# Memory values of a two-block transformer kernel: projection blocks 512 columns wide, into two PSUM banks

## The reference, cut

```python
def memory_cross_attention(x, mem_n, w_q, w_k, w_v, w_o):
    q = (x @ w_q).reshape(B, S, XA_HEADS, XA_DH)
    k = (mem_n @ w_k).reshape(B, -1, XA_HEADS, XA_DH)
    v = (mem_n @ w_v).reshape(B, -1, XA_HEADS, XA_DH)
    s = jnp.einsum('bshd,bmhd->bhsm', q, k).astype(jnp.float32) * (XA_DH ** -0.5)
    p = jax.nn.softmax(s, axis=-1).astype(x.dtype)
    o = jnp.einsum('bhsm,bmhd->bshd', p, v).reshape(B, S, D_MODEL)
    return o @ w_o
```

## Time and profile before

| | us |
|---|---|
| median of the runs (lowest, highest) | 1287.16 (1286.42, 1287.82) |
| profiled execution, its own time | 1286.86 |
| its span | 1284.8 |
| PE busy | 1267.4 (99%) |
| DVE busy | 829.8 (65%) |
| ACT busy | 661.7 (52%) |
| bytes read from HBM | 215.71 MB, 169 GB/s |

### The profile page before, as it was taken

How to read it: one execution, slowest core, us unless ns; L and a number is a source line. 1 busy time by engine, 2 the same in 40 slices (tenths; PEclk the granted TensorE clock), 3 DMA queues, 4 the chain that set the end, 5 groups by cost and what they waited for, 6 DMA issues and landing times.

```text
span 1284.8 us, 17262 instructions
## 1 busy us (share of the span) xinstructions
PE 1267.4 (99%) x6852; PEld 1093.4 (85%) x6852; DVE 829.8 (65%) x1269; ACT 661.7 (52%) x999; POOL 27.6 (2%) x32
## 2 busy tenths in 40 slices
PE   9999999999999999999999999999999999999997
PEld 8888888898788888899989997888888998888886
DVE  5655666878667565668988665755556564755554
ACT  6454546667574444453526644644445654644443
POOL 0000000010000000000000000000001000000000
PEclk9999999999999999999999999999999999999999
DMA  8655555452355555544424542655554442655551
GB/s 298 204 184 181 191 186 194 162 170 82 113 178 190 184 192 184 184 161 164 148 83 150 187 134 97 250 184 191 186 190 155 165 148 82 213 196 184 192 184 62
DMA packets 61854, 217.87 MB, mean 170 GB/s; under 512 B 6608, under 2 KB 9936, under 8 KB 61264
## 3 DMA queue, kind: packets, MB, share of 16 engines
q1 hardware_dynamic: 61488, 216.29, 50.2%
q10 hardware_dynamic: 288, 0.49, 0.1%
HBM read 215.71 MB, written 1.05 MB: 169 GB/s over the span
## 4 chain that ended last, share of the span: by engine, by line
PE 91%; DVE 6%; ACT 1%; DMA 1%; issue 0%; SPq 0%; POOL 0%; DVEq 0%; ACTq 0%
PE bank L1915 27%; PE bank L1917 26%; PE bank L1916 26%; DVE arena L1737 3%; DVE w_lo L1115 2%; PE bank L2117 1%; PE bank L1937 1%; PE bank L2254 1%; PE bank L2214 1%; PE bank L2003 1%; DMA w_raw<-weights_d 1%; PE bank L2225 1%; PE bank L2037 0%; PE bank L2246 0%; PE bank L2208 0%
## 5 line engine op out<-in xcount | busy, mean ns | idle before, releaser
L1115 DVE TENSOR_TENSOR w_lo<-w_raw,w_hi 128x1024 fp32r<-128x1024 f32 x383 | 467.6, 1226 | 343.7 <-ACT w_hi L583 342.3
L583 ACT ACTIVATE w_hi<-w_raw 128x1024 fp32r<-128x1024 f32 x383 | 404.1, 1059 | 475.6 <-PE bank L1917 454.8
L1915 PE MATMUL bank<-w_hi,x_hi 128*128 128x512 f32 (+2 forms) x928 | 361.3, 389 | 3.0 <-DVE w_lo L1115 2.4
L1917 PE MATMUL bank<-w_hi,x_lo 128*128 128x512 f32 (+2 forms) x928 | 356.6, 384 | 0.0
L1916 PE MATMUL bank<-w_lo,x_hi 128*128 128x512 f32 (+2 forms) x928 | 356.1, 384 | 0.0
L1915 PEld LDWEIGHTS bank<-w_hi,x_hi 128*128 128x128 f32 x928 | 175.1, 189 | 37.4 <-DVE w_lo L1115 3.6
L1917 PEld LDWEIGHTS bank<-w_hi,x_lo 128*128 128x128 f32 x928 | 175.1, 189 | 34.4
L1916 PEld LDWEIGHTS bank<-w_lo,x_hi 128*128 128x128 f32 x928 | 175.3, 189 | 32.6
L1915 PE MATMUL bank<-w_hi,h_hi 128*128 128x512 f32 (+1 forms) x364 | 142.4, 391 | 0.0
L1917 PE MATMUL bank<-w_hi,h_lo 128*128 128x512 f32 (+1 forms) x364 | 141.3, 388 | 0.0
L1916 PE MATMUL bank<-w_lo,h_hi 128*128 128x512 f32 (+1 forms) x364 | 141.3, 388 | 0.0
(11 more groups left out here) (312 smaller groups left out, 1440.0 us busy)
## 6 DMA issues: line engine op xcount, KB each, us to landing
w_raw<-weights_d SPq DMA_DIRECT2D x395, 512.0 KB, 3.3
arena<-weights_d SPq DMA_DIRECT2D x4, 512.0 KB, 6.2
arena<-ln_rows_d SPq DMA_DIRECT2D x2, 1024.0 KB, 5.5
arena<-late_d SPq DMA_DIRECT2D x1, 1056.0 KB, 5.7
xs<-x_d SPq DMA_DIRECT2D x2, 512.0 KB, 5.6
kv_mem<-mem_d SPq DMA_DIRECT2D x1, 1024.0 KB, 8.0
out_d<-xs SPq DMA_DIRECT2D x4, 256.0 KB, 2.4
cst<-cst_d SPq DMA_DIRECT2D x1, 671.0 KB, 7.2
```

The costliest lines, as they stand in the source:

```text
L583: nc.scalar.activation(w_hi[:, slot(b), :], w_raw[:, b % RAW, :], ACT.Copy).then_inc(hi_ready, 1)
L1115: nc.vector.tensor_tensor(w_lo[:, slot(b), :], w_raw[:, b % RAW, :], w_hi[:, slot(b), :].bitcast(F32), ALU.subtract).then_inc(lo_ready, 1)
L1915: nc.tensor.matmul(out, wh, xh, start=start, stop=False, skip_group_check=True)
L1917: return nc.tensor.matmul(out, wl, xh, start=False, stop=stop, skip_group_check=True)
```

## The change

The values are computed in blocks of 512 columns. A block now holds 2 x 128 rows of the inner length by 512 columns of weights, four blocks in a row (g = 0: m = 8 to 11, g = 1: m = 12 to 15) accumulate 512 of the 1024 value columns, for the two halves of the tokens in two banks, by 12 matmuls 512 columns wide per block instead of 24 of 256. ACT copies both banks after the fourth block (two copies of 128x512). The banks are 6 and 7, but 2 and 3 for g = 0 of layer 1. PE waits before the first block of a group: in layer 0 for mem_evac of 8 (all keys) and of 10 (both copies of g = 0), in layer 1 for g = 1 for both normalisations of layer norm 8. The query projection of layer 1 starts in bank 2 instead of 6, and waits at its start for 22 copies (before 23) and at c = 4 for 24 (before at c = 2). The row sums of the diff heads go to the second half of bank 5, ahead of weighted(5), and DVE reads them before head_lo(5). The host lays the weights of the values out to fit.

```diff
-        XQ_BANK = ((1, 3, 6, 7, 4, 5, 6, 7), (6, 3, 4, 5, 6, 7, 6, 7))
+        XQ_BANK = ((1, 3, 6, 7, 4, 5, 6, 7), (2, 3, 4, 5, 6, 7, 6, 7))
...
-        def fill_bank(l, m, k):
-
-            return PB[(2 if l == 1 and 8 <= m < 14 else 4 if l == 1 and m < 2 else 6) + k % 2]
+        def k_bank(l, m):
+
+            return PB[(4 if l == 1 and m < 2 else 6) + m % 2]
+
+        def v_bank(l, g):
+
+            return PB[2:4] if l == 1 and g == 0 else PB[6:8]
+
+        do_sums = PB[5][:, S:2 * S]
...
                     if m < DC:
                         done(b)
-                        nc.scalar.activation(k_mem[l][:, m, :], fill_bank(l, m, m)[:, 0:S], ACT.Copy).then_inc(mem_evac, 1)
-                    elif m % 2:
-                        c = (m - DC) // 2
+                        nc.scalar.activation(k_mem[l][:, m, :], k_bank(l, m)[:, 0:S], ACT.Copy).then_inc(mem_evac, 1)
+                    elif m % 4 == 3:
+                        g = (m - DC) // 4
                         done(b)
-                        nc.scalar.activation(v_mem[l][:, :, c * S:(c + 1) * S],
-                                             fill_bank(l, m, c)[:, :].rearrange("p (t n) -> p t n", n=S),
-                                             ACT.Copy).then_inc(mem_evac, 1)
+                        for t in range(2):
+                            nc.scalar.activation(v_mem[l][:, t, g * HALF:(g + 1) * HALF], v_bank(l, g)[t][:, :], ACT.Copy
+                                                 ).then_inc(mem_evac, 1)
...
+                if i == 8:
+                    dve.wait_ge(do_stat, 1)
+                    dve.wait_ge(o_ps, 6)
+                    dve.wait_ge(mla_hi, 2)
+                    link(nc.vector.tensor_scalar(rv[0:32, 0:S], do_sums[0:32, :], 1.0 / DIFF_V, RMS_EPS, ALU.mult, ALU.add))
+                    rsqrt_guess(rows[:, 0:S], rv[0:32, 0:S])
                 if i >= 3:
                     head_lo(i - 3, HEADS[i - 3])
-                if i == 8:
-                    dve.wait_ge(do_stat, 1)
-                    link(nc.vector.tensor_scalar(rv[0:32, 0:S], PB[6][0:32, 0:S], 1.0 / DIFF_V, RMS_EPS, ALU.mult, ALU.add))
-                    rsqrt_guess(rows[:, 0:S], rv[0:32, 0:S])
...
                     b = blk()
-                    o = m if m < DC else DC + (m - DC) // 2
-                    if o >= 2:
-                        pe.wait_ge(mem_evac, 12 * l + o - 1)
                     if m < DC:
-                        chunk(b, fill_bank(l, m, m)[:, 0:S], m_hi, m_lo)
-                    else:
-                        values(b, fill_bank(l, m, o), m % 2, m_hi, m_lo)
+                        if m >= 2:
+                            pe.wait_ge(mem_evac, 12 * l + m - 1)
+                        chunk(b, k_bank(l, m)[:, 0:S], m_hi, m_lo)
+                        continue
+                    g, i = (m - DC) // 4, m % 4
+                    if i == 0:
+                        pe.wait_ge(mem_evac, 12 * l + DC + (2 if l == 0 and g else 0))
+                        if l and g:
+                            pe.wait_ge(na_ready, 2 * LN[8] + 2)
+                            pe.wait_ge(nd_ready, 2 * LN[8] + 2)
+                    arrived(b)
+                    for k in range(2):
+                        for t in range(2):
+                            c, q, w = 2 * i + k, slice(t * P, (t + 1) * P), slice(k * HALF, (k + 1) * HALF)
+                            ins = three(v_bank(l, g)[t][:, :], m_hi[:, c, q], m_lo[:, c, q], w_hi[:, slot(b), w], w_lo[:, slot(b), w],
+                                        start=i == 0 and k == 0, stop=i == 3 and k == 1)
+                    ins.then_inc(block_done, 1)
...
-                pe.wait_ge(mem_evac, 19 if l == 0 else 23)
+                pe.wait_ge(mem_evac, 19 if l == 0 else 22)
                 for c in range(DC):
                     b = blk()
-                    if c == 3 - l:
+                    if c == 3 + l:
                         pe.wait_ge(mem_evac, 20 if l == 0 else 24)
...
+                if i == 7:
+                    for h in range(DIFF_HEADS):
+                        pe.wait_ge(do_sq, h + 1)
+                        ins = row_sums(do_sums[0:32, :], "rows_all", h, xs[:, h, 1, :], h == 0, h == DIFF_HEADS - 1)
+                    ins.then_inc(do_stat, 1)
                 if i >= 2:
                     weighted(i - 2, HEADS[i - 2])
-                if i == 7:
-                    pe.wait_ge(mem_evac, 11)
-                    for h in range(DIFF_HEADS):
-                        pe.wait_ge(do_sq, h + 1)
-                        ins = row_sums(PB[6][0:32, 0:S], "rows_all", h, xs[:, h, 1, :], h == 0, h == DIFF_HEADS - 1)
-                    ins.then_inc(do_stat, 1)
...
-    mem = [np.concatenate([columns(x["xa_wk_2"][l]), row_values(x["xa_wv_2"][l])]) for l in range(2)]
+    mem = [np.concatenate([columns(x["xa_wk_2"][l]), token_blocks(x["xa_wv_2"][l], HALF, 2).reshape(DC, P, BLK)]) for l in range(2)]
```

## The result

| | before | after |
|---|---|---|
| median of the runs beside each other, us | 1287.35 | 1291.68 |
| ratio (95% interval) | | 1.0035 (1.0024 to 1.0046) |
| span of the profiled execution, us | 1284.8 | 1289.9 |
| matmuls recorded on PE | 6852 | 6660 |

The account below looks back on a forecast made before the run. TensorE bounds the kernel, busy 1267.4 of 1284.8 us. Wait +5.15, blocks 12 to 15 -0.5, scores(8) -0.4, layer 1 -1.0, clock +1.5: +4.7 on 1287.16, so 1291.9 us, range 1289.4 to 1294.0.

Parts of the forecast that it names:

- The clock: Behind block 12's pause in layer 0, the granted clock falls to 0.50 for a while: 1.5 us lost.
- The wait at block 12: In layer 0, PE waits for both first-half copies, queued behind exponentials(3): idle about 5.7 us, block 12 starts 5.15 later.
- Nothing takes it up: During block 12's wait nothing else can run: PE is in order and later work queues behind it; delay 4.8 to 5.5 us.
- My bounds, 0.4 and 3: Clock loss after block 12's pause: near 0.4 us if slow time falls partly into it, near 3 if a second follows.
- The nines of the earlier trace: Profile page of the kernel before, read as TensorE at the full granted clock in all 40 slices.
- The wide matmuls: Value blocks of both layers: 0.13 us gained a block, 16 blocks, 2.1 us in all, ends 1.9 and 2.4.
- rival (c): Wide matmuls in the value blocks gain only about 0.03 us a block: +6.3, 1293.5 us; chance 0.05.
- slow first matmul of a group: Value blocks: a group's first matmul is slow, and a block standing alone pays it in either form; gain taken 0.13, not 0.15.
- L784's wait: Layer 0, scores(8): PE's 0.32 us idle on ACT's exponentials goes, as ACT no longer evacuates after block 13: -0.4 us.
- next late there is PE itself: At scores(8) of layer 0, once the wait on ACT's exponentials goes, PE is the next late: -0.4 us.
- Row sums and layer 1: Sums ahead of layer 0's weighted(5): cost 0, up to 0.5 without cover; layer 1's value blocks gain 1.0 us, layer-norm wait met.
- Rival (d): ACT evacuates block 11 ahead of exponentials(3): pause 1.4 us, sum -1.1, 1286.1; sign changes below a 2.5 us pause; chance 0.04.

Follow-up runs that it names:

- first and third experiments: First: kernel after, block 11's copies right behind exponentials(2), 1284.91 us. Third: kernel before, block 12 of layer 0 waiting for mem_evac 10 instead of 9, 1294.75 us.
- busy pause: Kernel after, with 42 unused 256-column matmuls on PE ahead of the wait at block 12 of layer 0: 1289.88 us, ratio 1.0018.
- sixth experiment: Kernel before, with only the diff heads' row sums moved ahead of weighted(5) and read on DVE ahead of head_lo(5): 1287.1 us, ratio 1.0006.
- block 12 later: Kernel after, with blocks 12 and 13 of layer 0 one turn later in the head loop (KV_FILL changed): 1288.13 us, ratio 1.0016.
- first four experiments: Kernel after with copies earlier, then with 42 matmuls in the pause; before with only the wait, then with only layer 1's wide blocks: 1284.91, 1289.88, 1294.75, 1285.47 us.

## Why the prediction was right

The time, 1291.68, is within 0.3 us of the 1291.9 forecast, and the mechanism is the one forecast. That it is so close is in part luck: the interval of the ratio runs from 3.1 to 5.9 us, and in the traces the change costs 6.42 us in layer 0 less 1.23 in layer 1, so 5.2, where 4.7 was forecast. The clock is the term that was too small.

- **The wait at block 12.** Forecast: idle 5.7 us, start 5.15 us later. Measured, less the 0.5 us of the start: 5.48 - 0.51 = 4.97 later, idle 5.13 in the row and some 5.3 by the starts (weighted(0)'s four matmuls begin at 295.17 and are 0.22 us apart). The idle time was off mainly because I took the time at which block 12 would start, 295.33, as the end of the work before it; weighted(0) fills PE for 0.2 us beyond that, and 0.35 in the modelled ends. The start was off by 0.18: 0.10 from the release, the rest from rounding and from copies that ended 0.04 earlier. The release took 0.05 us, as the earlier trace rows had it, not 0.15. The first and third experiments show the cause from both sides: with the copies earlier the pause is gone, and the wait alone brings it into a kernel that has nothing else of the change.
- **Nothing takes it up.** Right: +7.40 at block 13, and still +6.93 at the output projection, after all gains of layer 0.
- **The clock.** Forecast +1.5, measured 2.05 in the ledger and 1.8 by the busy pause. This is the term that was mis-sized: I priced a slow time as long as those of the earlier trace rows, 3.4 us. Here it began inside the pause and still lasted for 4.6 us of PE's work. My bounds, 0.4 and 3, hold it. Two readings behind this term don't stand. The nines of the earlier trace rows don't show a full clock throughout, as said above. And the length of the idle time was no sure guide even in the trace of before: its second spell, at 675.01, follows a wait of only 0.81 us, which I passed over. The last section comes back to this.
- **The wide matmuls.** Forecast 0.13 us a block with 0.15 as the plain difference of the rows; measured 0.13 in layer 0, where blocks stand alone, and 0.149 in layer 1. So rival (c) falls: the rows give 2 x 120.6 - 229 = 12.2 ns a pair. The Trainium skill (TensorE: Matmul & The Clock Gate, Back-to-back issue gap) states its fixed cost of 2.5 ns for the isolated gap of a single matmul. These fp32r matmuls, each with its own stationary load, don't agree with it as a price. The "slow first matmul of a group" of my reading isn't slow: weighted(0)'s last matmul starts at 295.82, block 12's first in the kernel before at 295.85 and its second at 296.15, and these 0.34 us are just the 0.22 of the one and the 0.12 of the other. The first starts early, it doesn't cost more.
- **L784's wait.** Forecast -0.4; it is gone from the waits, and scores(8) shows -0.50 with block 13's share in it. But 0.15 of it is given back by scores(9), so "next late there is PE itself" holds for part of it only.
- **Row sums and layer 1.** Forecast 0 and -1.0; measured 0 (sixth experiment) and -1.2. The layer norm's waits at block 12 don't appear in PE's view.
- **Rival (d)**, the evacuation ahead of exponentials(3), was worked out as 1286.1. Built in two places it gives 1285.93 behind head_out(0) and 1284.91 right behind exponentials(2). So the turning point, a pause of about 2.5 us, is the right scale: at 1.73 us the kernel can't be told from before (ratio 0.9987 to 1.0004).

## What to carry to other kernels

When two halves of a double buffer are joined into one, the copy that frees it becomes urgent, and its place in the copying engine's queue has to move with it: here the copies stood behind one head's softmax, which cost 5 us for a gain of 2, and moving that one step on ACT turned a loss of 0.35% into a gain of 0.18%. When a wait is added, follow the engine that must release it back through its own queue until a step that the waiting engine has issued; the sum of that chain is the pause. And price a pause of TensorE twice, once for its length and once for the lower clock that may follow.

## What the runs showed of the hardware

The lower clock after the long pause lasted twice as long as in the two spells near 644 and 675 us of the trace of before, 6.8 us against 3.4: from 299.1 to 305.9 us in the kernel after, 2.2 us of it inside the pause, and from 299.6 to 306.4, 1.5 us of it inside the pause, in the kernel with the wait alone. A shorter pause may or may not be followed by a fall, and its length doesn't tell. One wait stands in all nine traces, with the same instructions around it, PE for DVE's w_lo, 1.87 to 1.90 us long:

```profile
643.81 0.39 PE L1915 MATMUL bank<-w_hi,x_hi 128*128 128x256 f32 x1 [1.89 <-DVE w_lo L1115]
650.82 0.39 PE L1923 MATMUL bank<-w_hi,x_hi 128*128 128x256 f32 x1 [1.90 <-DVE w_lo L1121]
```

The first row is from the kernel before, where the clock falls at 644.3; the second is from the kernel after, where it stays up until 681.4. In the experiments it falls behind this wait in three (copies earlier, busy pause, block 12 later) and stays up in four. So how many spells a run meets varies, and the time with it: of the 27 runs of before beside the first four experiments, the four with a mean granted clock of 0.998 took 1285.1 to 1285.8 us, the ten with 0.995 took 1287.1 to 1289.4. Differences of a microsecond between medians of this kernel can be that alone.

At block 12 it is the same. In the profiled executions one pause of 1.73 us left the clock at 1.00, while two of 0.91 and 0.85 us, with scores(4) between, were followed by a fall at 298.95. The window rows of that kernel:

```profile
295.54:298.95 3.41, 1.65 (x8) 0.80 (x6) 3.31 (x16) 3.01 (x11) 0.00 (x0) 1.00 0.43 154
298.95:302.36 3.41, 3.41 (x10) 2.84 (x11) 3.31 (x9) 3.22 (x9) 0.00 (x0) 0.50 0.38 119
```

What decides it was not tried. Useless matmuls in the pause held the clock up, and were worth 1.8 us here, though not as much as removing the pause.
